# A transformer layer in split float32: projections over 512, 512 and 64 columns in place of 384, 384 and 320, and an output projection in two sums

## The reference

```
z = rmsnorm(x, g_mix) @ w_in                      # q, k, v; mLSTM inputs; gates
att = combine_groups(dilated attention ...)       # width 512
ml_h = mlstm over chunks of 128                   # width 512, gated by sigmoid(mo)
merged = concat(rmsnorm(att, g_attn_out), rmsnorm(gated ml_h, g_mlstm_out))
h1 = x + merged @ w_out                           # the output projection
h2 = h1 + cross_attention(rmsnorm(h1, g_cross)) @ w_co
y  = rmsnorm(h2 + (silu(hn @ w_gate) * (hn @ w_up)) @ w_down, g_final)
```

## Time and profile before

| what | value |
|---|---|
| median of 3 runs | 2271.48 us |
| the profiled execution, its own time | 2275.63 us |
| its span | 2273.7 us |
| PE busy | 1994.4 us (88%), 12998 matmuls |
| PEld busy | 1870.9 us (82%) |
| DVE busy | 958.5 us (42%) |
| ACT busy | 421.2 us (19%) |
| POOL busy | 58.3 us (3%) |
| mean granted TensorE clock | 0.939 |

### The profile page before, as it was taken

The page is one execution under the profiler, slowest core; times in us unless marked ns, Lnnn a source line. Parts: engine busy times, 40 slices in busy tenths (PEclk is TensorE's granted clock), DMA queues, the critical chain, the costliest instruction groups (busy, mean ns, idle before and its releaser), DMA issues.

```text
span 2273.7 us, 29921 instructions
## 1 busy us (share of the span) xinstructions
PE 1994.4 (88%) x12998; PEld 1870.9 (82%) x12998; DVE 958.5 (42%) x1627; ACT 421.2 (19%) x751; POOL 58.3 (3%) x68
## 2 busy tenths in 40 slices
PE   6998888998477693988998689899999999999995
PEld 5996558998367452888897579899999999999994
DVE  7223662246565444448224123534333333333344
ACT  2004660001321034203104310300000000000013
POOL 3000000000121000000000000000000000000000
PEclk8999999999688696998999999999999999999997
DMA  4206602110054484124203421111111111111112
GB/s 157 86 28 224 225 2 56 38 45 11 14 204 149 156 347 182 47 65 126 88 12 127 153 70 41 34 46 37 46 47 46 35 58 38 44 42 50 36 33 79
DMA packets 164993, 188.97 MB, mean 83 GB/s; under 512 B 15815, under 2 KB 153575, under 8 KB 160042
## 3 DMA queue, kind: packets, MB, share of 16 engines
q1 hardware_dynamic: 163370, 154.19, 20.9%
q10 hardware_dynamic: 1536, 33.56, 3.8%
HBM read 170.95 MB, written 50.33 MB: 97 GB/s over the span
## 4 chain that ended last, share of the span: by engine, by line
PE 49%; DVE 2%; ACT 2%; issue 1%; DVEq 1%; DMA 0%; ACTq 0%
PE psum L254 45%; PE psum L1557 1%; ACT scratch L1578 1%; PE psum L1674 1%; DVEq L184 1%; DVE weights_lo L211 0%; DVE scratch L1615 0%; PE psum L1687 0%; PE psum L1546 0%; ACT wide L1735 0%; PE psum L1711 0%; PE psum L302 0%; DVE weights_hi L209 0%; PE psum L1506 0%; PE psum L1537 0%
## 5 line engine op out<-in xcount | busy, mean ns | idle before, releaser
L254 PE MATMUL psum<-x_lo,weights_hi 128*128 128x384 f32 (+1 forms) x2328 | 517.1, 330 | 0.0
L254 PE MATMUL psum<-x_hi,weights_hi 128*128 128x384 f32 (+1 forms) x2136 | 477.5, 332 | 32.6 <-DVE x_lo L292 19.1
L254 PE MATMUL psum<-x_hi,weights_lo 128*128 128x384 f32 (+1 forms) x2136 | 473.8, 330 | 0.0
L209 DVE CAST weights_hi<-weights_raw 128x1024 fp32r<-128x1024 f32 (+2 forms) x144 | 94.5, 656 | 843.6 <-PE psum L254 832.0
L254 PEld LDWEIGHTS psum<-x_lo,weights_hi 128*128 128x128 f32 x2328 | 401.4, 189 | 0.0
L254 PEld LDWEIGHTS psum<-x_hi,weights_hi 128*128 128x128 f32 x2136 | 367.9, 189 | 38.0 <-issue 27.1
L254 PEld LDWEIGHTS psum<-x_hi,weights_lo 128*128 128x128 f32 x2136 | 367.7, 189 | 0.0
L211 DVE TENSOR_TENSOR weights_lo<-weights_raw,weights_hi 128x1024 fp32r<-128x1024 f32 (+2 forms) x144 | 165.8, 1151 | 4.9
L254 PE MATMUL psum<-hidden_hi,weights_hi 128*128 128x384 f32 x528 | 117.2, 330 | 1.9 <-DVE hidden_lo L1826 1.9
L254 PE MATMUL psum<-hidden_hi,weights_lo 128*128 128x384 f32 x528 | 116.8, 329 | 0.0
L254 PE MATMUL psum<-hidden_lo,weights_hi 128*128 128x384 f32 x528 | 116.8, 329 | 0.0
(11 more groups left out here) (302 smaller groups left out, 2195.8 us busy)
## 6 DMA issues: line engine op xcount, KB each, us to landing
work<-in_cache_win_k_dram SPq DMA_DIRECT2D x8, 2048.0 KB, 10.3
work<-in_cache_win_v_dram ACTq DMA_DIRECT2D x8, 2048.0 KB, 11.7
weights_raw<-in_w_in_dram SPq DMA_DIRECT2D x28, 512.0 KB, 3.8
weights_raw<-in_w_gate_dram SPq DMA_DIRECT2D x22, 512.0 KB, 3.8
weights_raw<-in_w_up_dram SPq DMA_DIRECT2D x22, 512.0 KB, 3.7
weights_raw<-in_w_down_dram SPq DMA_DIRECT2D x24, 384.0 KB, 3.3
weights_work<-in_cache_mem_k_dram SPq DMA_DIRECT2D x8, 1024.0 KB, 5.0
work<-in_cache_mem_v_dram SPq DMA_DIRECT2D x8, 1024.0 KB, 10.9
```

The lines of the kernel that those rows point to most:

```text
L209: nc.vector.tensor_copy(whi[:, w, 0:nk, :], raw[:, w, 0:nk, :]).then_inc(w_high, 1)
L254: mm = nc.tensor.matmul(PS[:, 3 * s + c, 0:n], w[:, s, k], x[part][:, k, t0:t0 + n], start=(k == 0 and w is whi and part == 0), stop=(k == ...
```

## The change

It has these parts.

1. `CHUNKS` is (512, 512, 64) in place of (384, 384, 320): the prompt's 1024 columns in two pieces, the 64 sample rows in a third. It is used by every projection over the 1088 columns and by the gates. The projections of the memory (256 columns) stay.
2. The output projection is summed in two halves of 4 k blocks in separate PSUM banks, mLSTM half first (banks 0 to 2), then the attention half (banks 3 to 5). Weights are applied to features that are scaled by the gain alone; VectorE multiplies each half's sum by its own inverse root when it takes it, and adds it to the residual. So the projection no longer waits for the norms. The barrier before it is gone.
3. GpSimd computes the squares of both halves ahead of time: those of the attention after prompt attention, those of the mLSTM during the cache stage. The sample columns of the attention are done by VectorE at the end.
4. Cache keys and values get three buffers each; key 2 is asked for before the state stores, value 0 at the stage's start. The residual's eight blocks and the first weights of the output projection are asked for within the cache stage.
5. Prompt attention runs one unit deeper: at step u scores of u, values of u-3, transpositions of u-2.

```diff
-CHUNKS = ((0, 384), (384, 384), (768, 320))
+CHUNKS = ((0, 512), (512, 512), (1024, 64))
...
-        def products(s, x, nk, chunks, before=lambda k: None):
+        def products(s, x, nk, chunks, before=lambda k: None, slot=None, k0=0):
...
+            slot = s if slot is None else slot
...
-                        mm = nc.tensor.matmul(PS[:, 3 * s + c, 0:n], w[:, s, k], x[part][:, k, t0:t0 + n],
+                        mm = nc.tensor.matmul(PS[:, 3 * s + c, 0:n], w[:, slot, k0 + k], x[part][:, k0 + k, t0:t0 + n],
...
-            for u in range(len(UNITS) + 2):
+            for u in range(len(UNITS) + 3):
                 if u < len(UNITS):
                     scores(u)
-                if u >= 2:
-                    values(u - 2)
-                if 1 <= u <= len(UNITS):
-                    turn(u - 1)
+                if u >= 3:
+                    values(u - 3)
+                if 2 <= u < len(UNITS) + 2:
+                    turn(u - 2)
...
+        def att_squares_pool(pool):
...
+            pool.wait_ge(o_taken, len(UNITS))
+            acc = att_sums[:, 0:SEQ]
+            chain(nc.gpsimd.tensor_tensor(acc, cat[:, 0, 0:SEQ], cat[:, 0, 0:SEQ], ALU.mult))
+            for k in range(1, NP):
+                chain(nc.gpsimd.tensor_tensor(att_square, cat[:, k, 0:SEQ], cat[:, k, 0:SEQ], ALU.mult))
+                last = nc.gpsimd.tensor_tensor(acc, acc, att_square, ALU.add)
...
         def win_load_first(sp):
             load_k(sp, 0)
             sp.wait_ge(phase_done, 4 * PH["sample"])
             load_k(sp, 1)
+            load_k(sp, 2)
...
+            load_v(act, 0)
             take_k(act, 0, 0)
...
+            ml_sums_tensor(pe)
             values(DB // 2 - 1)
             turn_o(DB // 2 - 1)
...
+        def out_loads(sp):
+            w = [w_view(A["w_out"])]
+            sp.wait_ge(wo_ready, 6)
+            proj_load(sp, w, 2, NB["out"])
...
+            for j in (0, 1, 2, 4, 5, 6, 7, 3):
...
+                sp.dma_start(XT[:, j, :], XT_DRAM[:, j * N:(j + 1) * N]).then_inc(xt_back[j // 4], 16)
+            proj_load(sp, w, 8, NB["out"], start=2)
+
+        def out_tensor_halves(pe):
...
+            for j in range(KB):
+                pe.wait_ge(w_split, n0 + j + 1)
+                if j:
+                    pe.wait_ge(ml_half_taken, j)
+                products(0, (xhi, xlo), NP, CHUNKS, (lambda k: None) if j else ml_first, (n0 + j) % 2, NP).then_inc(ml_half_ready, 1)
+                if j:
+                    pe.wait_ge(z_taken, n0 + j)
+                products(1, (xhi, xlo), NP, CHUNKS, (lambda k: None) if j else att_first, (n0 + j) % 2, 0).then_inc(z_ready, 1)
...
+        def out_vector_halves(dve):
+            chain, n0 = chains["dve"], NB["out"]
+            split_at(dve, n0)
+            for k in range(NP):
+                low(dve, sig_o, xhi[:, NP:], xlo[:, NP:], k, N, G_ML, J["ml"][2])
+            split_at(dve, n0 + 1)
+            for k in range(NP):
+                low(dve, cat, xhi, xlo, k, N, G_ATT, J["att"][2])
+            dve.wait_ge(rnorm_ready, J["ml"][1] + 1)
+            for j in range(KB):
+                split_at(dve, n0 + j + 2 if j + 2 < KB else NB["mk"] + j + 2 - KB) if j else None
+                dve.wait_ge(ml_half_ready, j + 1)
+                for c, (t0, w) in enumerate(CHUNKS):
+                    last = nc.vector.tensor_tensor(out_part[:, 0, t0:t0 + w], PS[:, c, 0:w], nr_ml[:, t0:t0 + w], ALU.mult)
+                last.then_inc(ml_half_taken, 1)
+                if j % 4 == 0:
+                    dve.wait_ge(xt_back[j // 4], 64)
+                dve.wait_ge(ml_half_taken, j + 1)
+                chain(nc.vector.tensor_tensor(XT[:, j], XT[:, j], out_part[:, 0], ALU.add))
+                if j == 0:
+                    split_at(dve, n0 + 2)
+                    dve.wait_ge(rnorm_ready, J["att"][1] + 1)
+                dve.wait_ge(z_ready, n0 + j + 1)
+                for c, (t0, w) in enumerate(CHUNKS):
+                    last = nc.vector.tensor_tensor(out_part[:, 1, t0:t0 + w], PS[:, 3 + c, 0:w], nr[:, t0:t0 + w], ALU.mult)
+                chain(last)
+                nc.vector.tensor_tensor(XT[:, j], XT[:, j], out_part[:, 1], ALU.add).then_inc(z_taken, 1)
+                if j:
+                    add_square(dve, nacc, j - 1, N, J["cross"][0])
```

More of the change, by code:

```diff
@@ L332, in lows @@
             return lambda k: pe.wait_ge(n_low, s0 + k + 1)
[L334 to L387, removed]
-            nc.vector.memset(SMALL[:, 41:42], 0.0).then_inc(norm_done, 1)
@@ L627, in att_vector @@
                 logits(u)
-                scale(u, 0)
-                if u >= 2:
-                    take(u - 2)
-                scale(u, 1)
+                if u:
+                    scale(u - 1, 0)
+                    scale(u - 1, 1)
+                if u >= 3:
+                    take(u - 3)
             last = len(UNITS) - 1
+            scale(last, 0)
+            scale(last, 1)
             dve.wait_ge(pt_ready, groups_to[last - 1, 0])
             nc.vector.memset(gate_w[:, :, :], 0.0).then_inc(gw_zeroed, 1)
-            take(last - 1)
-            take(last)
+            for u in (last - 2, last - 1, last):
+                take(u)
         def att_scalar(act):
@@ L1460, in win_vector, with ml_squares_pool @@
             output(DB // 2 - 1)
+        ml_sums, ml_square = cut(WRT, 4160, N), cut(WRT, 4160 + N, N // 2)
+        nr_ml, out_part = cut(HB, BIG, N), cut(HB, BIG + N, 2, N)
+        att_tail_square = cut(SC, 0, NP, NS)
+        ml_summed, att_tail_ready, ml_half_ready, ml_half_taken = (
+            sem("ml_summed"), sem("att_tail_ready"), sem("ml_half_ready"), sem("ml_half_taken"))
+        xt_back = [sem(f"xt_back{i}") for i in range(2)]
+        def ml_squares_pool(pool):
+            chain = chains["pool"]
+            pool.wait_ge(out_stored, 16 * mark["state"])
+            for t0 in (0, N // 2):
+                acc = ml_sums[:, t0:t0 + N // 2]
+                for k in range(NP):
+                    x = sig_o[:, k, t0:t0 + N // 2]
+                    if k == 0:
+                        last = nc.gpsimd.tensor_tensor(acc, x, x, ALU.mult)
+                    else:
+                        chain(nc.gpsimd.tensor_tensor(ml_square, x, x, ALU.mult))
+                        last = nc.gpsimd.tensor_tensor(acc, acc, ml_square, ALU.add)
+                    if k + 1 < NP or t0 == 0:
+                        chain(last)
+            last.then_inc(ml_summed, 1)
@@ new lines, in ml_sums_tensor, with ml_rnorm_scalar @@
+        def ml_sums_tensor(pe):
+            pe.wait_ge(ml_summed, 1)
+            for i, t0 in enumerate((0, HALF, SEQ)):
+                w = min(HALF, N - t0)
+                mm = nc.tensor.matmul(PS[:, 2 + i, 0:w], ONES[:, :], ml_sums[:, t0:t0 + w], start=True, stop=True)
+            mm.then_inc(bcast_ready, 1)
+        def ml_rnorm_scalar(act):
+            act.wait_ge(bcast_ready, J["ml"][1] + 1)
+            for i, t0 in enumerate((0, HALF, SEQ)):
+                w = min(HALF, N - t0)
+                last = nc.scalar.activation(nr_ml[:, t0:t0 + w], PS[:, 2 + i, 0:w], ACT.Ln, bias=EPSC[:, 0:1], scale=1.0 / AW)
+            chains["act"](last)
+            nc.scalar.activation(nr_ml, nr_ml, ACT.Exp, scale=-0.5).then_inc(rnorm_ready, 1)
```

194 lines of the change are left out of this document (105 added, 89 removed).

## The result

The changed kernel takes **2479.2 us** (median of 4 runs, 2477.4 to 2480.3), the kernel before in the same session 2272.3 us: ratio 1.0906, 95% interval 1.0893 to 1.0919. The forecast was 2454 us with a range of 2420 to 2497: right side, right mechanism, 25 us too low.

A forecast was written before the change was run, and what follows sets the result against it. Dense stretches were taken as bound by TensorE's matmul pace; 186.5 - 2 - 34.9 + 44.3 + 4.4 - 9 - 10 + 3 = +182.3 us on 2271.5 gave 2454 us, own range 2430 to 2480, with rivals 2420 to 2497.

The forecast's parts named there:

- The new triple: Projections over 1088 columns: three matmuls take 570 ns, +70; outside the output projection 2664 triples, +186.5 us.
- Load of plain f32 taken for fp32r: Narrow matmul's slot: a weight load of about 111 ns, seen for plain f32, was assumed for the projections' fp32r.
- The first rival: Narrow matmul costs only its columns: slot 40 ns, triple 499 ns, 2253 us; chance 4%.
- The second: Rival: load and exchange add up, wide slot 232 ns, narrow 120, triple 584, 2494 us; chance 14%.
- Entry: Before the output projection: the 40.0 us without the norms' wait shrink to 5.1, -34.9 us.
- Body: Output projection's matmuls: new triples, first-block sums, six pauses of 3.5 us and lower clock, 142.1 against 97.8, +44.3 us.
- End: After the output projection's last block: VectorE's remaining work takes 10.5 us against 6.1, +4.4 us.
- Cache stage: Cache stage: PE's waits for key 2 and the last values shrink, -9 us (bounds -18 and +2).
- I leave 7 us of the 11.8: Cache stage: of PE's 11.8 us wait for key 2, 7 remain through key 1's contention and key 3's lateness.
- Attention: Prompt attention: one unit more of distance cuts PE's waits for ScalarE's copies, 12.5 and 8.3 us; -10 us.
- GpSimd: Beside the gates: GpSimd's seven operations slow some 7 us of VectorE's work on PE's path, +3 us.
- No stalls: Rival: the output projection has no pauses, 29 us less than forecast, 2425 us; chance 6%.

The follow-up runs named there:

- the first experiment: The changed kernel with the pieces put back to 384, 384 and 320, all else kept: 2270.2 us, ratio 0.9981 to the kernel before.

## Why the prediction was right, and where it was short

- **The new triple.** Right in mechanism: the slot of 64 columns is the weight load's. Forecast 570 ns from 2 x 229.5 + 111, measured 573.4 from 2 x 232 + 109. I had two lines for the wide slot, 227 and 232, and took the middle; the upper one was right. 3.4 ns more for 2664 triples are 9 us, the difference of the first row of the table (8.3). This is one of the two terms that were short by most.
- **Load of plain f32 taken for fp32r.** The one thing I could not read from the trace before was whether the 110 ns of the earlier trace rows hold for the projections' own form. They do (108). The first rival (a slot of 40 ns, 2253 us) is refuted by the triple of 573 ns, by the 108 ns from load to load and by 128 columns costing the same slot as 64. The second (a narrow slot of 120 ns, a triple of 584) was right on the wide slot and wrong on the narrow one. Another form of adding up, load plus columns, is refuted by the 480, 480 and 128 columns, where it would have left the time near 2473.
- **Entry.** 5.1 forecast, 5.2 measured.
- **Body.** Pauses: forecast six of 3.5 us, found five of 3.54 and one of 3.89. The mis-sized term is what follows them. I priced the lower clock at up to 1.4 us a pause and put 8 for six, from the earlier trace rows, where old pieces ran 12 matmuls at half clock. Measured by moving the split: 16.2 us. Two causes, both in the traces: a new triple at the lower clock loses 1.07 - 0.57 = 0.49 us where an old one loses 0.41 (0.907 to 0.50); and the lower clock lasts longer. Behind the pause at 953.3 it holds for four triples, behind that at 972.4 for five, 5.3 us, and behind the other four for part of a sixth. With old pieces in the first experiment, five of the six pauses lose 1.5 to 1.6 us and one 2.8, already more than the 1.3 that I had put for each. The blocks between pauses take 15.5 to 16.8 us where 24 triples at full pace take 13.8. Body in all: 110.1 + 2.4 + 21.6 + 18.2, the last including the first block, as against 109.4 + 2.3 + 21 + 9.4 forecast.
- **End.** 10.5 forecast, a wait of 10.2 found.
- **Cache stage.** Here -9 was forecast and -4.7 measured. The step "I leave 7 us of the 11.8" left too little: 3.5 and 6.3 us remained, 9.8 in all. Key 1 came 3.5 us late, as expected; that value 0 is the reason is not shown, for no run asks for value 0 later. The other 6.3 stand in the profile as ScalarE's wait for the state stores, which I hadn't looked for. But key 3, which I had named, was late as well: with ScalarE's wait moved away the keys' waits were 9.3 us. Each of the two hides the other; before the change ScalarE's wait lay under the wait for key 2.
- **Attention.** -10 forecast, -8.1 by the trace, and undoing it costs 9: 8.3 fell to 3.2, 12.5 to 9.0, the drain took some back.
- **GpSimd.** +3 forecast, +1.6 found, and not where I had put it. Its seven operations ran from 355.4 to 371.8 us. Only the first met work of VectorE that PE waits for, the subtraction ahead of the gates' first matmul: 2.79 us instead of 1.22, and PE's pause there 3.82 instead of 2.25. With the old attention the pause is 3.83, with the new pieces alone, where GpSimd has nothing to do there, 2.25; so it is neither the depth nor the pieces. The gap between the gates and the next projection is 5.38 us in both kernels, and the +30.7 us of the gates' matmuls are explained by their triples. The 7 us of VectorE's work that I took to be on PE's path were some 1.2.
- **No stalls**, the third rival: refuted by the six pauses. The kernel with the pauses removed took 2442.3, 17 us over that rival's 2425; the triple and the cache stage give 12.6 of these.

## What to carry to other kernels

Where each matmul loads weights of its own, keep every column piece long enough to cover one load, and divide the columns evenly before dividing them by meaning; pieces of 512, 320 and 256 were as good as 384, 384 and 320, pieces with a 64 cost 9%. In an engine that frees another's PSUM banks, put nothing ahead of that work which waits for something later: here one line in the wrong order cost 37 us, nearly half of it in clock after the pauses. Before a wait is removed, list who waits for the same event; a wait that a longer one covered takes its place.

## What was unexpected of the hardware

- The floor of a matmul with its own 128 by 128 weights, from load to load, is 108 to 110 ns at the full clock for 64 and 128 columns, and 210 ns at the lower one. It was measured for fp32r, and for f32 in the earlier trace rows. It doesn't show in the start of the next matmul, 30 and 60 ns behind, but in that of the one after it.
- Wide slots carry an overhead over their columns at 2.4 GHz: 512 columns 230 to 235 ns (213 of columns), 480 columns 216 to 222 (200), 256 columns 120 (107). At the lower clock it nearly vanishes: 512 columns in 427 to 430 ns, which is 427 of columns, and an old triple takes 0.907 us, exactly its 1088 columns at 1.2 GHz.
- A pause of 3.5 us costs 5.5 us with the old pieces and 6.3 with the new ones, when what the clock takes afterwards is counted.
- A subtraction of VectorE over 128 by 1024 took 2.79 us with an operation of GpSimd beside it that had started 0.49 us earlier, and 1.22 without one.
